# Retention values with tokens as rows: 512-column matmuls on the weights in place of transposes, and one summed square per head

## The reference

```python
def _retention(xn, w_in, subln, w_out):          # H=4 heads, Dk=256, Dv=512, chunks of 128
    q, k, v, g = split(xn @ w_in, ...)           # 1024, 1024, 2048, 2048 columns
    ...
        att = einsum('bhqd,bhkd->bhqk', qq, kk) * decay_intra
        o = (einsum('bhqk,bhkv->bhqv', att, vv) + einsum('bhqd,bhdv->bhqv', qq, R) * xi)
    ...
    o = _rms(o, subln).reshape(B, T, H * Dv)     # one mean square per token and head, 512 values
    return (silu(g) * o) @ w_out
```

## Time and profile before

| | |
|---|---|
| median of 3 runs | 2315.48 us |
| profiled execution | 2315.99 us, of which 2314.2 us are the span of the trace |
| PE, DVE, ACT, POOL busy | 98%, 64%, 52%, 12% |
| mean granted TensorE clock | 0.99 |
| the retention phase | from 1914 to about 2127 us of the span |

### The profile page before, as it was taken

The page is one execution under the profiler, slowest core; times in us unless marked ns, Lnnn a source line. Parts: engine busy times, 40 slices in busy tenths (PEclk is TensorE's granted clock), DMA queues, the critical chain, the costliest instruction groups (busy, mean ns, idle before and its releaser), DMA issues.

```text
span 2314.2 us, 48858 instructions
## 1 busy us (share of the span) xinstructions
PE 2271.9 (98%) x18466; PEld 2256.5 (98%) x18466; DVE 1475.1 (64%) x2279; ACT 1201.2 (52%) x1743; POOL 275.2 (12%) x326
## 2 busy tenths in 40 slices
PE   8999999999999999999999999899999999999999
PEld 8999999999999999999999998789999999999999
DVE  5655877665566469776657647866646656675663
ACT  5444676544444358755445536655445544465552
POOL 1001461100100126130020010020010010001000
PEclk9999999999999999999999999989999999999999
DMA  6555424555455443355645654335655655445563
GB/s 218 172 192 162 138 101 147 166 179 187 159 172 192 162 166 109 129 175 188 198 157 190 202 171 148 101 125 184 197 166 190 199 173 168 146 159 179 188 203 125
DMA packets 100401, 386.58 MB, mean 167 GB/s; under 512 B 11312, under 2 KB 12464, under 8 KB 100304
## 3 DMA queue, kind: packets, MB, share of 16 engines
q1 hardware_dynamic: 99648, 383.89, 50.4%
q0 software_dynamic: 368, 1.26, 0.2%
q10 hardware_dynamic: 288, 0.12, 0.0%
HBM read 384.18 MB, written 1.05 MB: 166 GB/s over the span
## 4 chain that ended last, share of the span: by engine, by line
PE 91%; DVE 5%; ACT 3%; issue 1%; POOL 0%; DMA 0%; SPq 0%; ACTq 0%; POOLq 0%
PE bank L328 29%; PE bank L330 29%; PE bank L329 29%; DVE wlo L345 1%; ACT whi L338 1%; PE bank L623 1%; PE bank L593 1%; PE bank L720 1%; PE bank L638 1%; PE bank L846 0%; ACT dp L1083 0%; DVE dsc L1480 0%; DMA raw<-w 0%; PE bank L856 0%; DVE qk L1313 0%
## 5 line engine op out<-in xcount | busy, mean ns | idle before, releaser
L328 PE MATMUL bank<-u_hi,whi 128*128 128x256 f32 (+1 forms) x3968 | 1137.7, 287 | 7.8 <-DVE u_lo L378 7.2
L330 PE MATMUL bank<-u_hi,wlo 128*128 128x256 f32 (+1 forms) x3968 | 1131.5, 285 | 0.0
L329 PE MATMUL bank<-u_lo,whi 128*128 128x256 f32 (+1 forms) x3968 | 1131.1, 285 | 0.0
L345 DVE TENSOR_TENSOR wlo<-raw,whi 128x1024 fp32r<-128x1024 f32 (+1 forms) x680 | 883.4, 1301 | 214.2 <-ACT whi L338 213.1
L338 ACT ACTIVATE whi<-raw 128x1024 fp32r<-128x1024 f32 (+1 forms) x680 | 746.3, 1111 | 281.4 <-PE bank L330 276.5
L328 PEld LDWEIGHTS bank<-u_hi,whi 128*128 128x128 f32 x3968 | 753.2, 190 | 8.8 <-DVE wlo L345 7.2
L330 PEld LDWEIGHTS bank<-u_hi,wlo 128*128 128x128 f32 x3968 | 753.5, 190 | 0.0
L329 PEld LDWEIGHTS bank<-u_lo,whi 128*128 128x128 f32 x3968 | 750.6, 189 | 0.7
L330 PE MATMUL bank<-hid_hi,wlo 128*128 128x256 f32 (+1 forms) x1408 | 400.6, 285 | 0.0
L328 PE MATMUL bank<-hid_hi,whi 128*128 128x256 f32 (+1 forms) x1408 | 399.4, 284 | 0.0
L329 PE MATMUL bank<-hid_lo,whi 128*128 128x256 f32 (+1 forms) x1408 | 398.1, 283 | 0.0
(11 more groups left out here) (252 smaller groups left out, 2082.0 us busy)
## 6 DMA issues: line engine op xcount, KB each, us to landing
raw<-w SPq DMA_DIRECT2D x552, 512.0 KB, 3.4
raw<-w SPq DMA_DIRECT2D x128, 704.0 KB, 4.6
h<-xT SPq DMA_DIRECT2D x4, 272.0 KB, 5.1
outT<-h SPq DMA_DIRECT2D x8, 128.0 KB, 4.6
consts<-cst POOLq DMA_DIRECT2D x1, 576.0 KB, 4.0
dist<-cst POOLq DMA_DIRECT2D x1, 192.0 KB, 2.7
rdist<-cst POOLq DMA_DIRECT2D x1, 192.0 KB, 3.2
sgain<-small POOLq DMA_DIRECT2D x1, 145.5 KB, 3.8
```

The lines of the kernel that those rows point to most:

```text
L328: pe.matmul(out, w_h, x_hi, start=first, stop=False)
L329: pe.matmul(out, w_h, x_lo, start=False, stop=False)
L330: return pe.matmul(out, w_l, x_hi, start=False, stop=last)
L345: dve.tensor_tensor(wlo[:, n % RING, 0:COLS[n]], raw[:, n % RING, 0:COLS[n]], whi[:, n % RING, 0:COLS[n]], ALU.subtract).then_inc(lo_ready, 1)
```

## The change

The v panels are turned round: the host lays the weights of a head's v out as four panels of 2 x (128 x 512), the activations become the stationary operand and the weights stream past as 512 columns. So v arrives in banks 2 and 3 with tokens as rows, and the transposes, the tile `rv` and its 16 evacuations on DVE go. A factor per token is then a factor per partition: two small float32 matmuls (of 2 columns) in the first head's q panels and a logarithm and an exponential on ACT make `rR`, which ACT's copy (`scale=`) and DVE's subtraction apply. The mean square now comes from one float32 matmul: POOL first adds the squares, 512 columns and then 256 (`rosum`), and PE waits for the second sum (`r_osq_step`).

```diff
-ACCS = {"ffn": 2 * FT, "mix": 36 + 16, "da": 24, "rt": 48, "final": 0}
+ACCS = {"ffn": 2 * FT, "mix": 36 + 16, "da": 24, "rt": 32, "final": 0}
-FOUR_BANKS = 8 * (RT_HEADS + 1)
+FOUR_BANKS = 4 * RT_HEADS + 8
...
-rv = sb("rv", [128, 4, SEQ], f32, area)
+rR = sb("rR", [128, 4], f32, area)
...
+rosum = sb("rosum", [128, 3, SEQ], f32, area)
...
+        def rt_acc(t, c):
+return 4 * t + c if t < RT_HEADS else 4 * RT_HEADS + 8 * (t - RT_HEADS) + c
...
 def rt(y):
     b = BASE[y]
+    def v_panel(hd, q):
+        n = b["P"] + 8 * hd + 4 + q
+        pe.wait_ge(lo_ready, n + 1)
+        if q == 0 and hd >= 1:
+            pe.wait_ge(r_v_ready, 2 * hd)
+        for kk in range(2):
+            k = 2 * q + kk
+            w_h, w_l = (w[:, n % RING, 512 * kk:512 * kk + 512] for w in (whi, wlo))
+            for i in range(2):
+                tok = slice(META + 128 * i, META + 128 * i + 128)
+                pe.matmul(bank[2 + i][:, :], u_hi[:, k, tok], w_h, start=(k == 0), stop=False)
+                pe.matmul(bank[2 + i][:, :], u_lo[:, k, tok], w_h, start=False, stop=False)
+                mm = pe.matmul(bank[2 + i][:, :], u_hi[:, k, tok], w_l, start=False, stop=(k == KD - 1))
+                if k == KD - 1 and i == 0:
+                    mm.then_inc(r_vt_full, 1)
+        mm.then_inc(panel_used, 1)
     for t in range(RT_HEADS + 2):
         for c in range(8):
-            in_panel2(y, 8 * t + c)
+            if t < RT_HEADS and c >= 4:
+                v_panel(t, c - 4)
+            else:
+                in_panel2(y, 8 * t + c, rt_acc(t, c))
...
+            if t == 0 and c == 1:
+                for i in range(2):
+                    mm = pe.matmul(bank[6][:, 2 * i:2 * i + 2], ssq[:, META + 128 * i:META + 128 * i + 128],
+                                   mean_d[:, 0:2], start=True, stop=True, skip_group_check=True)
+                mm.then_inc(r_R_full, 1)
...
             if c == 0:
-                pe.wait_ge(a_evac, b["A"] + 8 * t)
-                if hd >= 1:
-                    pe.wait_ge(r_v_ready, 2 * hd)
-                for i in range(2):
-                    for f in range(4):
-                        mm = pe.transpose(bank[2 + i][:, f * 128:f * 128 + 128],
-                                          rv[:, f, 128 * i:128 * i + 128], ident)
-                    mm.then_inc(r_vt_full, 1)
                 pe.wait_ge(r_qk_ready, hd + 1)
...
             if c == 7:
-                pe.wait_ge(r_osq, hd + 1)
+                pe.wait_ge(r_osq_step, 2 * (hd + 1))
                 if hd >= 1:
                     pe.wait_ge(r_ro_done, hd)
-                for f in range(4):
-                    mm = pe.matmul(bank[7][:, 0:SEQ], mean_512, rosq[:, f, :], start=(f == 0),
-                                   stop=(f == 3))
-                mm.then_inc(r_osum, 1)
+                pe.matmul(bank[7][:, 0:SEQ], mean_512, rosum[:, 2, :], start=True,
+                          stop=True).then_inc(r_osum, 1)
...
+            if t == 0 and c == 2:
+                act.wait_ge(r_R_full, 1)
+                act_rsqrt(act, rR[:, :], bank[6][:, 0:4], rms_eps, r_R_log, 1, r_R_ready)
...
-                    act.activation(rv_hi[:, i, :], bank[2 + i][:, :], ACT.Copy).then_inc(r_v_hi, 1)
+                act.activation(rv_hi[:, 0, :], bank[2][:, :], ACT.Copy, scale=rR[:, 0:1]).then_inc(r_v_hi, 1)
+                act.wait_ge(panel_used, P + 8 * t)
+                act.activation(rv_hi[:, 1, :], bank[3][:, :], ACT.Copy, scale=rR[:, 2:3]).then_inc(r_v_hi, 1)
...
-            elif c >= 4:
-                dve.tensor_tensor(rv[:, c - 4, :], src, R[:, W], ALU.mult).then_inc(a_evac, 1)
...
-                    dve.tensor_tensor(rv_lo[:, i, :], bank[2 + i][:, :], rv_hi[:, i, :],
-                                      ALU.subtract).then_inc(r_v_ready, 1)
+                    dve.scalar_tensor_tensor(out=rv_lo[:, i, :], in0=bank[2 + i][:, :],
+                                             scalar=rR[:, 2 * i:2 * i + 1], in1=rv_hi[:, i, :],
+                                             op0=ALU.mult, op1=ALU.subtract).then_inc(r_v_ready, 1)
...
+    if kind == "rt":
+        for hd in range(RT_HEADS):
+            pool.wait_ge(r_osq, hd + 1)
+            pool.tensor_tensor(rosum[:, 0:2, :], rosq[:, 0:2, :], rosq[:, 2:4, :], ALU.add)\
+                .then_inc(r_osq_step, 1)
+            pool.wait_ge(r_osq_step, 2 * hd + 1)
+            if hd >= 1:
+                pool.wait_ge(r_osum, hd)
+            pool.tensor_tensor(rosum[:, 2, :], rosum[:, 0, :], rosum[:, 1, :], ALU.add)\
+                .then_inc(r_osq_step, 1)
```

More of the change, by code:

```diff
@@ L311, in build @@
         r_osq, r_osum, r_ro_done, r_on_done = (sem(s) for s in ("r_osq", "r_osum", "r_ro_done", "r_on_done"))
+        r_R_full, r_R_log, r_R_ready, r_osq_step = (
+            sem(s) for s in ("r_R_full", "r_R_log", "r_R_ready", "r_osq_step"))
         r_silu, r_p_done, r_y_hi, r_y_ready = (sem(s) for s in ("r_silu", "r_p_done", "r_y_hi", "r_y_ready"))
@@ L689, in mix, with in_panel2 @@
                          KD * (l + 1), N2)
-            def in_panel2(y, j):
+            def in_panel2(y, j, acc=None):
                 b = BASE[y]
+                acc = j if acc is None else acc
                 pe.wait_ge(lo_ready, b["P"] + j + 1)
-                pe.wait_ge(a_evac, b["A"] + j - (1 if j < FOUR_BANKS + 2 else 3))
+                pe.wait_ge(a_evac, b["A"] + acc - (1 if acc < FOUR_BANKS + 2 else 3))
                 for k in range(KD):
@@ L698, in in_panel2 @@
                         pe.wait_ge(u_ready, u_base(y) + (KD - 2 if k == 0 else k + 1))
-                    mm = products(pe, bank[panel_bank(j)][:, 0:SEQ], (b["P"] + j) % RING, k, u_hi[:, k, META:T],
+                    mm = products(pe, bank[panel_bank(acc)][:, 0:SEQ], (b["P"] + j) % RING, k, u_hi[:, k, META:T],
                                   u_lo[:, k, META:T], k == 0, k == KD - 1)
@@ L814, in rt @@
                         if c == 0:
-                            pe.wait_ge(a_evac, b["A"] + 8 * t)
-                            if hd >= 1:
-                                pe.wait_ge(r_v_ready, 2 * hd)
-                            for i in range(2):
-                                for f in range(4):
-                                    mm = pe.transpose(bank[2 + i][:, f * 128:f * 128 + 128],
-                                                      rv[:, f, 128 * i:128 * i + 128], ident)
-                                mm.then_inc(r_vt_full, 1)
                             pe.wait_ge(r_qk_ready, hd + 1)
-                            if hd >= 1:
+                            if hd == 0:
+                                pe.wait_ge(r_R_log, 1)
+                            else:
                                 pe.wait_ge(r_at_done, hd)
@@ L1148, in rt @@
                         if t < RT_HEADS and c == 3:
-                            act.wait_ge(a_evac, A + 8 * t + 4)
+                            act.wait_ge(a_evac, A + rt_acc(t, c) + 1)
                             act.activation(rqk_hi[:, t % 2, :, :], rqk[:, t % 2, :, :], ACT.Copy).then_inc(r_qk_hi, 1)
@@ L1154, in rt @@
                         if c == 0:
-                            for i in range(2):
-                                act.wait_ge(r_vt_full, 2 * hd + i + 1)
-                                act.activation(rv_hi[:, i, :], bank[2 + i][:, :], ACT.Copy).then_inc(r_v_hi, 1)
+                            if hd == 0:
+                                act.wait_ge(r_R_ready, 1)
+                            act.wait_ge(r_vt_full, hd + 1)
+                            act.activation(rv_hi[:, 0, :], bank[2][:, :], ACT.Copy, scale=rR[:, 0:1]).then_inc(r_v_hi, 1)
+                            act.wait_ge(panel_used, P + 8 * t)
+                            act.activation(rv_hi[:, 1, :], bank[3][:, :], ACT.Copy, scale=rR[:, 2:3]).then_inc(r_v_hi, 1)
                         if c == 1:
@@ L1162, in rt @@
                             act.wait_ge(r_o_done, 2 * (hd + 1))
+                            if hd >= 1:
+                                act.wait_ge(r_osq_step, 2 * hd)
                             act.activation(rosq[:, :, :], ro[:, 4 * hd:4 * hd + 4, :], ACT.Square).then_inc(r_osq, 1)
@@ L1523, in rt @@
                         j = 8 * (t - RT_HEADS) + c
-                        src = bank[panel_bank(8 * t + c)][:, 0:SEQ]
-                        dve.wait_ge(panel_used, P + 8 * t + c + 1)
+                        src = bank[panel_bank(rt_acc(t, c))][:, 0:SEQ]
                         if t >= RT_HEADS:
+                            dve.wait_ge(panel_used, P + 8 * t + c + 1)
                             dve.tensor_tensor(rg[:, c % 2, :], src, R[:, W], ALU.mult).then_inc(a_evac, 1)
-                        elif c >= 4:
-                            dve.tensor_tensor(rv[:, c - 4, :], src, R[:, W], ALU.mult).then_inc(a_evac, 1)
-                        else:
+                        elif c < 4:
+                            dve.wait_ge(panel_used, P + 8 * t + c + 1)
```

(7 more changed lines are left out.)

3 lines of the change are left out of this document (2 added, 1 removed).

## The result

The kernel after takes 2319.74 us (median of 16 runs, 2317.69 to 2323.73) against 2315.38 us of the kernel before on the same chip (16 runs). The medians are 4.4 us apart; the ratio on record is 1.0022, 95% interval 1.0015 to 1.0028, so the change is slower, by a little. The forecast was +7.2 us, 2322.6, with a range of 2311 to 2332.

The account below looks back on a forecast made before the run. PE, busy for 98% of the span and never waiting in the phase, was taken as the bound: savings -10.4, waits +10.8, clock +6.8 make +7.2 us, so 2322.6 us; range 2311 to 2332, the forecast's own 2318 to 2327.5.

Parts of the forecast that it names:

- What PE is spared: PE's savings over four heads: transposes 3.5 us, mean square 5.2, turned v panels 2.2, less 0.45 for two small matmuls.
- The bound at which nothing is gained: Turned v matmuls of 512 columns: at 236 ns each, time on top of the columns grows with them; 0 us spared.
- the middle that I chose: Turned v matmuls of 512 columns: 224.7 ns each, 2.2 us spared, between nothing and 3.9 us.
- The wait: At each head's mean square, PE waits 2.7 us for POOL's two adds, 10.8 us in four heads.
- the hold-up: POOL's second add is held back by DVE's split for panel 6, and takes about 1.6 us.
- The clock: After each head's wait, one stretch at 1.2 instead of 2.4 GHz: 1.7 us a head, 6.8 us; bounds 0 to 13.6.
- a sign of being wrong: Listed signs: PE's wait under 1.5 us, clock at 1.00 behind it, or adds done before PE arrives.
- the clock holds: Rival: behind the waits the clock stays up or falls in one head of four; 2315.9 to 2317.6 us, chance 0.20.
- the prediction's own border of 2320.1: Upper border of counting as the same, about 0.2% (4.6 us) from no change; slower 0.62, same 0.27, faster 0.11.
- POOL losing twice: Rival: second add also waits for panel 7's split, wait 3.9 us; 2329.5 to 2334.3 us; chance 0.16, shared with longer clock falls.
- The adds did not fit ahead of the split: Rival "faster": POOL's adds end before DVE's panel 6 split, or wait about 1.3 us; 2308.6 to 2310.3 us, chance 0.14.
- the turned panels cost more: Rival on the v panels: 236 ns a matmul, 2.2 us less spared; moves any case by 1.4 us, no chance of its own.

Follow-up runs that it names:

- the kernel before that one: The changed kernel with the mean's matmul behind the next head's first panel and the norm's steps on DVE and ACT moved later too: 2311.31 us, ratio 0.9987.

## Why the prediction was right

- **What PE is spared.** Forecast 3.5 + 2.2 - 0.45 = 5.25 us for the turned v; the phase of that kernel alone is 4.6 shorter. The transposes' 3.5 and the mean's 5.2 stand: the kernel with the mean moved has both, and its phase is 9.1 shorter. That is 4.6 + 5.2 = 9.8, less some 0.4 for its wait of 0.15 and 0.3 by which its output projection is longer than that of the turned v alone; there, at 2073.42, a weight load waits 0.23 us for DVE's `ry_lo`. The term that was mis-sized is the turned matmul: 231.9 ns where I took 224.7, so 192 x (236.2 - 231.9) = 0.8 us spared instead of 2.2. The 4.6 comes as near to 5.25 as it does only because the output projection gave 0.5 us that nobody had forecast: with the right step the sum was 3.85. The bound at which nothing is gained, by which the time on top belongs to the columns, was nearer to the truth than the middle that I chose.
- **The wait.** Forecast 2.7 us a head; measured 2.23, 2.23, 2.22 and 2.44, and 0.25 more that PE loses at each and that no wait shows: 2.5 us, 10 us in all for the forecast's 10.8. Its steps held one by one: the first add took 1.27 (1.33 forecast), the hold-up made the second 1.59 (1.6), and the split beside the first add took 1.47 (1.5), both splits together 3.13. POOL's sum was there 3.03 us after the squares' end (3.09 forecast), and PE would have come to the mean 0.69 after it (0.53), as its matmuls were slower; both make the wait shorter. PE's last v matmul ends some 0.8 us after the squares do, and POOL needs 3 us.
- **The rule on the port.** The second add took 1.59 us beside a split instead of 0.74. In the kernel with the first add twice DVE's two splits took 1.3 us more than where POOL is still (3.67 for 2.35). The Trainium skill ("SBUF — State Buffer", Who interferes with whom) has a DVE instruction with two SBUF inputs and a POOL instruction that reads SBUF exclude each other; these rows agree. The forecast without it, a wait of 1.85, is excluded by the four of 2.2 and more: with 0.74 for the second add the listed wait would have been 1.4.
- **The clock.** Forecast 1.7 us in each head, 6.8; measured 1.7 in three of four, 5.1. Behind the second head's wait the clock stayed at 1.00, which the prediction names as a sign of being wrong. In the kernel with POOL's sum only it fell in one of four. The rival "the clock holds" would have given 2315.9 to 2317.6 and was wrong in size but not in kind: among waits of this length the clock fell behind some and not behind others. So this term is right in part by luck. With one fall instead of three the profiled phase would have been only 1.6 to 1.9 us longer than before.
- **The sum.** -9.8 + 10 + 5.1 = +5.3 us, where the phase shows +5.0 and the medians +4.4. The forecast was a small difference of large terms, each of which came out somewhat smaller than forecast; the result lies in the forecast's own range from 2318 on, but by the prediction's own border of 2320.1 it is still within what it counts as the same.
- **The other rivals.** POOL losing twice did not happen: its second add got in between the two splits, as at 930.7. The adds did not fit ahead of the split. That the turned panels cost more was right in its direction: 192 x (231.9 - 224.7) = 1.4 us less was spared.

What stays open is why the clock held behind the second head's wait and fell behind the first's and third's of the same length. No run was made to tell.

## What to carry to other kernels

A sum that is moved from the busiest engine to an idle one is worth what it saves only if its result is there when the busy engine comes: read the slack at that place first (here 0.8 us against 2.9 of adds), and if it isn't enough, move the consumer behind the next piece of work instead of shortening the adds. Leave everything else at its place when doing so. In an in-order queue the mean one panel later turned +4.4 us into -10.1, with the same instructions. The norm that was moved along in the kernel before that one gave about half of the gain back.

## What was not expected of the hardware

- The time on top of a matmul's columns grows with the columns: the step is 118.1 ns for 256 (118.6 for the halves of the turned matmuls) and 231.9 for 512, at a granted clock of 1.00. By these two, of the 11.4 ns over 256 columns at 2.4 GHz some 7 belong to the columns.
- The same matmuls of 256 columns in the output projection step by 120.0 ns in the two kernels with v as before and by 118.7 with the turned v, at a granted clock of 1.00. Why stays open.
- A wait costs PE about 0.25 us beyond the idle time that is listed (0.27 and 0.26 at waits of 2.1 and 2.2 us).
- In this phase waits of 0.15 to 0.8 us (thirteen, in four kernels) never took the clock down, those of 2.1 to 2.4 us did in four of eight, and one of 2.96 and four of 3.8 to 4.4 us always did.
- An add of 512 columns takes POOL 1.27 us and DVE 0.69; 256 columns take 0.74 and 0.42.
